# GLA decode moved three weight slabs forward, and the head norm spread over six gate slabs, in a one-core hybrid decoder step

## The chip, the cores and the metric

The kernel runs on one core of a Trainium2 chip. The metric is the device time of one execution in microseconds (us). The kernel before takes 2381.51 us, the median of three runs (2378.88 to 2381.75).

## What is computed

One layer of a hybrid decoder on 280 token columns: 256 prompt tokens, 8 sample tokens (one new token for each of 8 sequences) and 16 meta tokens. A half-step SwiGLU FFN, then two branches side by side, gated linear attention (GLA) and sliding-window attention, merged by two sigmoid gates, then a second FFN. What the change touches is GLA for the 8 sample tokens, and the norm behind it:

```python
# per sample token and head: one step of the recurrence on a state S (128 x 256), read and written back
S = S * exp(logg)[..., None] + k[:, None] * v[None, :]
o = q @ S
# head norm, gain, and gate r, for all tokens
of = o * lax.rsqrt(mean(o * o, axis=-1, keepdims=True) + EPS) * onorm
of = of * silu(r)
gla_b = of @ w_o
h = h + (sigmoid(ga + ba) * gla_b + sigmoid(gb + bb) * swa_b) @ w_out
```

All products with weights are done in three single-pass products of split operands (high times high, low times high, high times low).

## The kernel before

The work is a sequence of 404 weight **slabs**, one per 128 output columns, handled in a fixed order written out by hand for each engine. SyncE loads a slab's weights (1 MB, 16 tiles of 128x128) into one of two `raw` buffers. ScalarE rounds them to `w_hi` (`split_hi`, L458); VectorE subtracts to get `w_lo` (`split_lo`, L799); TensorE does 32 matmuls with `w_hi` (L1226, L1227: the high pass) and 16 with `w_lo` (L1232: the low pass); VectorE takes the result out of PSUM and frees the bank. There are two buffers of each kind, so the split for slab n+2 can only start when slab n has been multiplied:

```python
def split_hi(half, b, kt, first=False):          # called with half + 1 while slab (half, b) runs
    act.wait_ge(raw_loaded[b], 16 * (half + 1))
    if not first:
        act.wait_ge(slab_done, 2 * half + b - 1)
    act.activation(w_hi[:, b, 0:kt * P], raw[:, b, 0:kt * P], ACT.Copy).then_inc(hi_split, 1)
```

In the middle of the kernel stand 28 slabs that I number e = 8 to 35, as the changed code does. e = 8 to 15 are the rest of the GLA gate `ga`; e = 16 to 23 the output gate `r` (ScalarE `gate_r`, VectorE `silu_r`); e = 24 to 31 eight slabs of the merge gate `gb`; e = 32 to 35 four more. Then come twelve MERGE1 slabs, each half from the sliding-window output and half from the GLA output in `y3_hi`, `y3_lo`.

Beside e = 8 to 20 runs the chunked GLA of the prompt. Its small matmuls are issued by TensorE between the high and the low pass of a slab (`work_between`). ScalarE copies transposed value and key rows out of PSUM (`value_rows` L654, `key_rows` L658) and VectorE updates the state (`new_state` L1059, at e = 12, 17 and 20; semaphore `g_S` reaches 10 after the third).

The decode of the 8 sample tokens starts after slab e = 23. TensorE transposes the sample values (L1547), ScalarE and VectorE split them into `v_split`, and then token u goes beside slab e = 24 + u:

- ScalarE `pick_token` (L704) makes a selection tile for the token, one token ahead; L721 scales the four head states by the decay.
- TensorE broadcasts the token's values into two PSUM banks just before the slab (L1569, two matmuls of 512 columns). It waits there for the token's pick (`n_pick`) and for the state update of token u - 1 (`n_state`).
- VectorE adds key times value (L1103).
- TensorE multiplies state u by the query during the next slab (`decode_outputs` L1558, 8 products of one column), spread over the high pass; ScalarE copies the 8 columns out (L724).
- GpSimd loads and stores the 512 KB states, three buffers in turn (L418, L407).

After the last token ScalarE squares the outputs (L734). TensorE sums the squares over partitions in the slab e = 32 (L1583, L1584). ScalarE takes roots (L742), VectorE reciprocals (L1136) and the product with gain (L1118). GpSimd multiplies with `r` (L433). ScalarE and VectorE split the result into `y3_hi` (L747, L752) and `y3_lo` (L1124), which MERGE1 reads.

Of the kernel before, what the change touches and what calls it, by code (L numbers as in the profile page):

```python
# [21 lines left out]
ALU = mybir.AluOpType  # L22
# [5 lines left out]
P = 128  # L28
# [33 lines left out]


# [3 lines left out]
def build_layer(nc, t):  # L67
    ctx = ExitStack()
    with ctx:
# [16 lines left out]
        v_split, pick = small_r[0:32 + NS, 0:8 * P], small_r[0:32 + NS, 8 * P:].rearrange("p (a b) -> p a b", a=2)  # L86
# [93 lines left out]
        def by_block(a, h, side, n):  # L180
# [4 lines left out]
        S0 = R[:, 2112:2112 + 3 * GH * DV].rearrange("p (n h v) -> p n h v", n=3, h=GH)  # L185

        osq = [proj[:, 0:4, 0:TR], at(5216, 4, TR)]
        ostd, ors = at(4160, GH, TR), at(2112, GH, TR)
        ow, rsum = at(5216, 4, TR), proj[:, 0:4, 0:TR]
# [39 lines left out]
        state_out, nv_tr, nv_zero, nv_hi, nv_lo = (  # L229
            sem(n) for n in ("state_out", "nv_tr", "nv_zero", "nv_hi", "nv_lo"))  # L230
# [7 lines left out]
        on_sq, on_sum, on_std, on_rs, on_w, on_g, ohi_done, olo_done = (  # L238
            sem(n) for n in ("on_sq", "on_sum", "on_std", "on_rs", "on_w", "on_g", "ohi_done", "olo_done"))
# [36 lines left out]
        N_CONST = 10  # L276
# [3 lines left out]
        def _(sp):  # L280
# [19 lines left out]
            for dst, name in ((ones, "c_ones"), (ident, "c_ident"), (gbias, "gbias"),  # L300
                              (onorm, "onorm"), (nslope, "c_nslope"),
                              (a_bias, "a_bias"), (sink_bh, "sink_bh"), (pick_scale, "c_pick")):
                sp.dma_start(dst[:], t[name]).then_inc(consts_loaded, 16)
# [34 lines left out]
        def _(pool):  # L338
# [3 lines left out]
            for i in range(LEVELS):  # L342
# [6 lines left out]
                                   channel_multiplier=-1).then_inc(mask_fill, 1)  # L349

# [53 lines left out]
            def store_state(u):  # L404
                pool.wait_ge(n_state, 4 * (u + 1))
                pool.wait_ge(n_o, u + 1)
                pool.dma_start(t["state_s"][u], S0[:, u % 3]).then_inc(s0_stored[u % 3], 16)  # L407

            pool.wait_ge(g_chunk, 1)
            pool.dma_start(S0[:, 0], t["state_in"][0]).then_inc(s0_loaded[0], 16)  # L410
            pool.wait_ge(g_S, 10)
            pool.dma_start(t["state_p"], S).then_inc(state_out, 16)
            pool.wait_ge(state_out, 16)
            for u in range(1, NS):
                b = u % 3
                if u >= 3:
                    pool.wait_ge(s0_stored[b], 16 * (u // 3))
                pool.dma_start(S0[:, b], t["state_in"][u]).then_inc(s0_loaded[b], 16)  # L418
                if u >= 2:
                    store_state(u - 2)  # L420
# [32 lines left out]
        def _(act):  # L453
# [217 lines left out]
            for e in range(8, 24):  # L671
                half, b = GATE_A + e // 2, e % 2
                split_hi(half + 1, b, KD)
                act.wait_ge(bank_free, 2 * half + b + 1)
                if e < 16:
                    gate_a(half, slice(e, e + 1))
                else:
                    gate_r(e - 16)
                if e == 10:
                    for q in range(2):  # L680
                        value_rows(0, q)
                    key_rows(0)
                if e in (13, 14):
# [9 lines left out]
                if e == 19:  # L693
                    out_tiles(1)


            def gate_b(m):
                act.activation(merged[:, m], merged[:, m], ACT.Sigmoid, bias=gbias[:, 1, m:m + 1]).then_inc(sigb_done, 1)

            def pick_token(u):  # L700

                if u >= 2:
                    act.wait_ge(n_vbc, u - 1)
                act.activation(pick[:, u % 2], ones[0:32 + NS, :], ACT.Copy,  # L704
                               scale=pick_scale[0:32 + NS, u:u + 1]).then_inc(n_pick, 1)

            act.activation(v_split.rearrange("p (a b) -> p a b", a=8),
                           ones[0:32 + NS, :].unsqueeze(1).broadcast_to([32 + NS, 8, P]), ACT.Copy,
                           scale=0.0).then_inc(nv_zero, 1)
# [999 lines left out]
```

## Time and profile before

| | |
|---|---|
| median of 3 runs | 2381.51 us |
| profiled execution: its own time, its span | 2381.69 us, 2379.9 us |
| TensorE busy | 2335.3 us, 98% of the span |
| VectorE, ScalarE, GpSimd busy | 1290.0, 913.1, 165.7 us |
| mean granted TensorE clock | 0.987 |

Times in the profile are microseconds from the start of the span. PE is TensorE's matmul, DVE VectorE, ACT ScalarE, POOL GpSimd. The profile gives for every instruction its line, its start and duration, and, in brackets, how long the engine sat idle before it and which instruction ended that. PE's matmuls are pipelined, so their durations overlap; what counts is the distance between starts. The granted clock is the share of TensorE's full 2.4 GHz; 0.50 is its lower level, 1.2 GHz.

### The profile page before, as it was taken

How to read it: one execution, taken by the hardware profiler on the slowest of the kernel's cores; microseconds unless marked ns; L12 is line 12 of the kernel's file. 1: busy time of each engine (PE TensorE's matmuls, PEld its weight loads, DVE VectorE, ACT ScalarE, POOL GpSimd, SP SyncE). 2: the span in 40 equal slices, each digit the busy share in tenths (PEclk: the TensorE clock that was granted, in tenths of full speed). 3: DMA queues.
4: the chain of work that ended last, by engine and by line, in shares of the span. 5: the costliest groups of instructions: out<-in, count | busy, mean ns of one | idle time of the engine just before them, and what ended most of it. 6: DMA issues, size and time to landing. Idle time of an engine off the chain costs nothing.

```text
span 2379.9 us, 45022 instructions
## 1 busy us (share of the span) xinstructions
PE 2335.3 (98%) x18348; PEld 2302.7 (97%) x18348; DVE 1290.0 (54%) x1435; ACT 913.1 (38%) x935; POOL 165.7 (7%) x190
## 2 busy tenths in 40 slices
PE   8999999999999999999998989999999999999997
PEld 8999999999999999889998989999999999999997
DVE  6555554555555745554445565655555555555555
ACT  5333333333333434445234533443333333333332
POOL 0000000000000600001000120220000000000017
PEclk9999999999999999998899999999999999999999
DMA  5445444544544544335234545454455455545444
GB/s 204 174 152 183 176 160 161 191 161 159 188 163 158 183 163 160 109 127 191 95 132 181 203 149 179 175 179 176 174 177 192 176 170 192 183 161 195 177 171 147
DMA packets 66870, 401.56 MB, mean 169 GB/s; under 512 B 8530, under 2 KB 11218, under 8 KB 31456
## 3 DMA queue, kind: packets, MB, share of 16 engines
q1 hardware_dynamic: 61712, 385.73, 46.2%
q0 software_dynamic: 4032, 13.74, 1.7%
q8 instruction: 54, 0.88, 0.1%
q10 hardware_dynamic: 1056, 1.08, 0.1%
q14 instruction: 16, 0.13, 0.0%
HBM read 391.24 MB, written 9.27 MB: 168 GB/s over the span
## 4 chain that ended last, share of the span: by engine, by line
PE 95%; DVE 2%; ACT 1%; issue 1%; POOL 1%; DMA 0%; DVEq 0%; SPq 0%; ACTq 0%; POOLq 0%
PE bank L1226 30%; PE bank L1232 30%; PE bank L1227 30%; ACT w_hi L458 1%; DVE w_lo L799 1%; PE bank L1445 1%; PE bank L1365 0%; POOL scratch L433 0%; PE bank L1558 0%; PE bank L1363 0%; PE bank L1431 0%; PE bank L1430 0%; PE bank L1411 0%; DVE scratch L1136 0%; PE bank L1569 0%
## 5 line engine op out<-in xcount | busy, mean ns | idle before, releaser
L458 ACT ACTIVATE w_hi<-raw 128x2048 fp32r<-128x2048 f32 (+1 forms) x404 | 705.6, 1746 | 1274.5 <-PE bank L1232 1231.3
L799 DVE TENSOR_TENSOR w_lo<-raw,w_hi 128x2048 fp32r<-128x2048 f32 (+1 forms) x404 | 844.5, 2090 | 469.5 <-ACT w_hi L458 469.5
L1226 PE MATMUL bank<-x_hi,w_hi 128*128 128x264 f32 (+1 forms) x3440 | 886.0, 292 | 1.0 <-DVE x_lo L1165 1.0
L1227 PE MATMUL bank<-x_lo,w_hi 128*128 128x264 f32 (+1 forms) x3440 | 878.2, 289 | 0.0
L1226 PEld LDWEIGHTS bank<-x_hi,w_hi 128*128 128x128 f32 x3440 | 652.2, 190 | 11.6 <-issue 7.1
L1227 PEld LDWEIGHTS bank<-x_lo,w_hi 128*128 128x128 f32 x3440 | 652.1, 190 | 0.1
L1226 PE MATMUL bank<-y_hi,w_hi 128*128 128x264 f32 (+1 forms) x2368 | 597.8, 287 | 6.4 <-DVE y_lo L1124 5.9
L1227 PE MATMUL bank<-y_lo,w_hi 128*128 128x264 f32 (+1 forms) x2368 | 596.2, 287 | 0.0
L1232 PE MATMUL bank<-x_hi,w_lo 128*128 128x264 f32 (+1 forms) x3440 | 469.8, 288 | 0.0
L1226 PEld LDWEIGHTS bank<-y_hi,w_hi 128*128 128x128 f32 x2368 | 446.8, 189 | 7.7 <-DVE y_lo L1124 7.1
L1227 PEld LDWEIGHTS bank<-y_lo,w_hi 128*128 128x128 f32 x2368 | 447.5, 189 | 0.0
L1232 PEld LDWEIGHTS bank<-x_hi,w_lo 128*128 128x128 f32 x3440 | 445.5, 188 | 0.2
L1232 PE MATMUL bank<-y_hi,w_lo 128*128 128x264 f32 (+1 forms) x2368 | 322.5, 286 | 0.0
L1232 PEld LDWEIGHTS bank<-y_hi,w_lo 128*128 128x128 f32 x2368 | 303.2, 189 | 0.0
L858 DVE SCALAR_TENSOR_TENSOR hT<-bank,hT 128x280 f32 (+3 forms) x128 | 56.4, 441 | 116.9 <-PE bank L1232 116.6
L353 POOL MEMSET scratch<- 128x280 f32 x3 | 1.0, 334 | 1584.3 <-DVE scratch L831 1465.1
L831 DVE TENSOR_TENSOR scratch<-bank,rstd 128x280 f32<-128x280 f32 (+1 forms) x88 | 38.8, 441 | 129.5 <-PE bank L1232 129.5
L825 DVE TENSOR_TENSOR scratch<-bank,rstd 128x280 f32<-128x280 f32 (+1 forms) x88 | 38.8, 441 | 117.5 <-PE bank L1232 117.5
L359 POOL TENSOR_TENSOR scratch<-scratch 128x264 f32<-128x264 f32 (+1 forms) x47 | 74.4, 1583 | 3.7
L894 DVE SCALAR_TENSOR_TENSOR proj<-bank,rstd 128x280 f32<-128x280 f32 (+1 forms) x28 | 12.4, 442 | 58.5 <-PE bank L1232 58.4
L834 DVE TENSOR_TENSOR scratch<-scratch 128x280 f32<-128x280 f32 (+1 forms) x88 | 38.8, 441 | 3.0
L829 DVE TENSOR_TENSOR scratch<-scratch 128x280 f32<-128x280 f32 (+1 forms) x88 | 38.3, 436 | 1.0 <-ACT scratch L483 1.0
(252 smaller groups left out, 905.1 us busy)
## 6 DMA issues: line engine op xcount, KB each, us to landing
raw<-in_w_in SPq DMA_DIRECT2D x176, 1024.0 KB, 4.8
raw<-in_w_out SPq DMA_DIRECT2D x128, 704.0 KB, 4.1
raw<-in_w_proj SPq DMA_DIRECT2D x52, 1024.0 KB, 4.8
raw<-in_w_merge SPq DMA_DIRECT2D x32, 1024.0 KB, 4.8
raw<-in_w_o SPq DMA_DIRECT2D x16, 1024.0 KB, 4.8
scratch<-in_state_in POOLq DMA_DIRECT2D x8, 512.0 KB, 6.1
out_state_s<-scratch POOLq DMA_DIRECT2D x8, 512.0 KB, 5.3
hT<-in_xT SPq DMA_DIRECT2D x4, 560.0 KB, 7.3
```

What stands on the lines that cost most here:

```text
L359: pool.tensor_tensor(acc[:, 0:T], acc[:, 0:T], sq[:, 0:T], ALU.add).then_inc(acc_done, 1)
L458: act.activation(w_hi[:, b, 0:kt * P], raw[:, b, 0:kt * P], ACT.Copy).then_inc(hi_split, 1)
L799: dve.tensor_tensor(w_lo[:, b, 0:kt * P], raw[:, b, 0:kt * P], w_hi[:, b, 0:kt * P].bitcast(F32), ALU.subtract).then_inc(lo_split, 1)
L825: dve.tensor_tensor(a_n[:, 0:T], bank[own][:, 0:T], rstd[:, 0:T], ALU.mult).then_inc(bank_free, 1)
L829: dve.tensor_tensor(act_a[:, 0:T], a_n[:, 0:T], sig[:, 0:T], ALU.mult).then_inc(acta_done, 1)
L831: dve.tensor_tensor(b_n[:, 0:T], bank[own + 1][:, 0:T], rstd[:, 0:T], ALU.mult).then_inc(bank_free, 1)
L834: dve.tensor_tensor(s32[:, 0:T], act_a[:, 0:T], b_n[:, 0:T], ALU.mult).then_inc(s_done, 1)
L858: dve.scalar_tensor_tensor(hT[:, m, 0:T], bank[b][:, 0:T], 0.5, hT[:, m, 0:T], ALU.mult, ALU.add).then_inc(bank_free, 1)
L1226: pe.matmul(out, w, x[0][:, k, 0:T], start=(k == ks[0]), stop=False)
L1227: pe.matmul(out, w, x[1][:, k, 0:T], start=False, stop=False)
L1232: last = pe.matmul(out, w_lo[:, b, k * P:(k + 1) * P], x[0][:, k, 0:T], start=False, stop=(k == ks[-1]))
L1445: last = pe.matmul(bank[4 if i % 2 else 7][:, n * CK:(n + 1) * CK].rearrange("p (b x) -> p b x", x=h), proj[:, GK + g, c * CP:(c + 1) * CP ...
```

## The change

- **Start.** The loops over e = 8 to 23, over tokens and over the last four gate slabs become one loop over e = 8 to 35 on each engine. Token u now goes beside slab e = 21 + u (`DECODE = 21`).
- **Sample value rows.** The transposed tile of the meta tokens (columns 152 to 279) also holds the sample tokens, in partitions 104 to 111; at e = 10 it is split from there into `v_split`, now 128 partitions. The eight transposes L1547 go, and the `c_pick` table is made by three GpSimd instructions and no longer loaded.
- **ScalarE's order in a slab.** Decay of token u, then the weight split, then row copies, picks and outputs, then the gate.
- **States.** The three state buffers lie apart and are loaded as soon as their space is free.
- **Norm.** Token outputs are done in one piece between the passes. Each head's two squares are added on VectorE first, so TensorE's sums halve. They are done at e = 30, and roots, reciprocals, products and splits are spread over e = 30 to 35.

First, ScalarE beside a decode slab. Before (L698 gate, L704 pick, L721 decay, L724 token output, L458 weight split):

```order
L698 ACTIVATE proj<-proj,gbias 128x264 [waits bank_free]
L704 ACTIVATE small_r<-ones,pick_scale 40x128 [waits n_vbc]
L721 ACTIVATE scratch<-scratch,a_smp 128x256 [waits s0_loaded2]
L721 ACTIVATE scratch<-scratch,a_smp 128x256 x3
L724 ACTIVATE scratch<-bank 128x8 [waits n_o]
L458 ACTIVATE w_hi<-raw 128x2048 [waits slab_done,raw_loaded0]
L698 ACTIVATE proj<-proj,gbias 128x264 [waits bank_free]
```

And in the change (L695 decay, L465 weight split, L690 pick, L699 token output, L679 gate):

```order
L695 ACTIVATE scratch<-scratch,a_smp 128x256 [waits s0_loaded0]
L695 ACTIVATE scratch<-scratch,a_smp 128x256 x3
L465 ACTIVATE w_hi<-raw 128x2048 [waits slab_done,raw_loaded0]
L690 ACTIVATE small_r<-ones,pick_scale 128x128 [waits n_vbc]
L699 ACTIVATE scratch<-bank 128x8 [waits n_o]
L679 ACTIVATE proj<-proj,gbias 128x264 [waits bank_free]
```

The pick for the next token stood ahead of the weight split, which waits for the running slab, and now stands behind it.

Second, TensorE where the decode begins. Before, at the end of e = 23 (L1232 low pass, L1547 transposes of the sample values, L1569 broadcast of the first token's values):

```order
L1232 MATMUL bank<-x_hi,w_lo 128x264 [waits lo_split]
L1232 MATMUL bank<-x_hi,w_lo 128x264 x15
L1547 MATMUL bank<-ident,proj 8x128 [waits g_S,g_vtok]
L1547 MATMUL bank<-ident,proj 8x128 x7
L1569 MATMUL bank<-small_r 128x512 [waits n_pick,nv_lo]
L1569 MATMUL bank<-small_r 128x512
```

And in the change, at the end of e = 20 (L1503 keys by values for the last prompt chunk, L1248 low pass, L1573 broadcast):

```order
L1503 MATMUL bank<-scratch 128x256 [waits g_S,g_vtok,g_ktok]
L1503 MATMUL bank<-scratch 128x256 x3
L1248 MATMUL bank<-x_hi,w_lo 128x264 [waits lo_split]
L1248 MATMUL bank<-x_hi,w_lo 128x264 x15
L1573 MATMUL bank<-small_r 128x512 [waits g_S,nv_lo,n_pick]
L1573 MATMUL bank<-small_r 128x512
```

The transposes are gone, and the first broadcast, now three slabs earlier, waits itself for `g_S`. VectorE makes that count there, in the change, right behind its part of slab e = 20 (L1131 evacuation, L811 weight split, L1071 the third `new_state`, L1078 and L1080 `silu_r`):

```order
L1131 TENSOR_TENSOR r_act<-bank,rstd 128x264 [waits slab_done,rlo_done]
L811 TENSOR_TENSOR w_lo<-raw,w_hi 128x2048 [waits hi_split]
L1071 SCALAR_TENSOR_TENSOR scratch<-scratch,a_chunk,bank 128x256 [waits g_S,g_o,g_chunk,g_kv]
L1071 SCALAR_TENSOR_TENSOR scratch<-scratch,a_chunk,bank 128x256 x3
L1078 TENSOR_TENSOR r_act<-r_act,gadT 128x264 [waits r_sig]
```

This order is as before; only what waits for it has moved. The core of the diff:

```diff
+DECODE, NORM = 21, 30
...
# ScalarE
-            for e in range(8, 24):
+            for e in range(8, 36):
                 half, b = GATE_A + e // 2, e % 2
+                u = e - DECODE
+                if 0 <= u < NS:
+                    decay_state(u)
                 split_hi(half + 1, b, KD)
-                act.wait_ge(bank_free, 2 * half + b + 1)
-                if e < 16:
-                    gate_a(half, slice(e, e + 1))
-                else:
-                    gate_r(e - 16)
...
                 if e == 18:
                     for q in range(2):
                         value_rows(2, q)
                     key_rows(2)
                 if e == 19:
+                    act.wait_ge(pick_fill, 3)
+                    pick_token(0)
                     out_tiles(1)
+                if 0 <= u < NS - 1:
+                    pick_token(u + 1)
+                if 0 < u <= NS:
+                    token_out(u - 1)
+                if u == NS:
+                    head_squares()
+                if e == NORM:
+                    head_roots()
+                if e > NORM + 1:
+                    branch_hi(e - NORM - 2)
                 act.wait_ge(bank_free, 2 * half + b + 1)
-                gate_b(8 + u)
+                if e < 16:
+                    gate_a(half, slice(e, e + 1))
+                elif e < 24:
+                    gate_r(e - 16)
+                else:
+                    gate_b(8 + e - 24 if e < 32 else 4 + e - 32)
...
# VectorE, behind the evacuation and split of each slab
+                if e == NORM - 1:
+                    head_sums()
+                if e in (NORM, NORM + 1):
+                    for g in range(2):
+                        head_inverse(2 * (e - NORM) + g)
...
+                    gated_norm(e - NORM)
+                if e > NORM + 1:
+                    branch_lo(e - NORM - 2)
+                    if e - NORM < GH:
+                        gated_norm(e - NORM)
...
# TensorE, between the passes of a slab
+                    if DECODE < e <= DECODE + NS:
+                        for n in range(8):
+                            decode_outputs(e - DECODE - 1, n)
+                    if e == NORM:
+                        head_norms()
...
+            def broadcast_values(u):
+
+                pe.wait_ge(n_pick, u + 1)
+                if u == 0:
+                    pe.wait_ge(nv_lo, 2)
+                    pe.wait_ge(g_S, 10)
+                else:
+                    pe.wait_ge(n_state, 4 * u)
...
+            for e in range(8, 36):
+                if DECODE <= e < DECODE + NS:
+                    broadcast_values(e - DECODE)
+                slab(GATE_A + e // 2, e % 2, KD, x, TR, beside=work_between(e))
```

## Rows read from the trace of the kernel before

**Rows 1.** The page: the chain that ended last, shares by engine.

```profile
PE 95%; DVE 2%; ACT 1%; issue 1%; POOL 1%; DMA 0%; DVEq 0%; SPq 0%; ACTq 0%; POOLq 0%
```

**Rows 2.** Waits of TensorE, whole span: us in total, times, longest.

```profile
PE bank L1226 <- DVE y_lo L1124: 5.9, 3, 3.6
PE bank L1500 <- ACT scratch L654: 2.4, 1, 2.4
PE bank L1342 <- ACT scratch L574: 2.3, 1, 2.3
```

**Rows 3.** Timeline, PE: first matmuls of slabs e = 19, 20, 21 (start, duration).

```profile
1227.24 0.28 PE L1226 MATMUL bank<-x_hi,w_hi 128*128 128x264 f32 x1
...
1240.87 0.28 PE L1226 MATMUL bank<-x_hi,w_hi 128*128 128x264 f32 x1
...
1248.43 0.28 PE L1226 MATMUL bank<-x_hi,w_hi 128*128 128x264 f32 x1
```

**Rows 4.** Timeline, DVE: evacuations of e = 15, 16, 23, 24, 25; split and new_state in e = 20.

```profile
1203.28 0.43 DVE L1075 TENSOR_TENSOR proj<-bank,rstd 128x264 f32<-128x264 f32 x1 [1.28 <-PE bank L1232]
...
1212.72 0.43 DVE L1075 TENSOR_TENSOR r_act<-bank,rstd 128x264 f32<-128x264 f32 x1 [5.14 <-PE bank L1232]
...
1250.64 2.29 DVE L799 TENSOR_TENSOR w_lo<-raw,w_hi 128x2048 fp32r<-128x2048 f32 x1 [1.51 <-ACT w_hi L458]
1252.85 1.65 DVE L1059 SCALAR_TENSOR_TENSOR scratch<-scratch,a_chunk,bank 128x256 f32<-128x256 f32 x4
...
1266.29 0.43 DVE L1075 TENSOR_TENSOR r_act<-bank,rstd 128x264 f32<-128x264 f32 x1 [0.37 <-PE bank L1232]
...
1283.53 0.43 DVE L1107 TENSOR_TENSOR proj<-bank,rstd 128x264 f32<-128x264 f32 x1 [5.74 <-PE bank L1232]
...
1292.00 0.43 DVE L1107 TENSOR_TENSOR proj<-bank,rstd 128x264 f32<-128x264 f32 x1 [2.60 <-PE bank L1232]
```

**Rows 5.** Timeline, ACT: split and row copies at e = 18; pick; split at e = 30.

```profile
1227.50 1.92 ACT L458 ACTIVATE w_hi<-raw 128x2048 fp32r<-128x2048 f32 x1 [0.54 <-PE bank L1232]
...
1232.45 1.06 ACT L654 ACTIVATE scratch<-bank 128x512 f32<-128x512 f32 x2
...
1328.18 0.39 ACT L704 ACTIVATE small_r<-ones,pick_scale 40x128 fp32r<-40x128 f32 x1
...
1334.43 1.91 ACT L458 ACTIVATE w_hi<-raw 128x2048 fp32r<-128x2048 f32 x1 [1.91 <-PE bank L1232]
```

**Rows 6.** Timeline, PE: the first broadcast, and the one before slab e = 31.

```profile
1274.88 1.22 PE L1569 MATMUL bank<-small_r 40*128 40x512 f32 x2 [7.82 <-DVE small_r L1096]
...
1334.26 0.73 PE L1569 MATMUL bank<-small_r 40*128 40x512 f32 x2
1334.92 0.39 PE L1226 MATMUL bank<-x_hi,w_hi 128*128 128x264 f32 x1
```

**Rows 7.** Timeline, PE: the last token's outputs, then starts up to the third MERGE1 slab.

```profile
1342.65 1.84 PE L1558 MATMUL bank<-proj,scratch 128*128 128x1 f32 x16
...
1350.29 0.61 PE L1583 MATMUL bank<-proj,ones 128*128 128x264 f32 x2
...
1353.65 0.48 PE L1226 MATMUL bank<-x_hi,w_hi 128*128 128x264 f32 x1
...
1365.57 0.28 PE L1226 MATMUL bank<-x_hi,w_hi 128*128 128x264 f32 x1
...
1371.44 0.28 PE L1226 MATMUL bank<-y_hi,w_hi 128*128 128x264 f32 x1
...
1393.01 0.28 PE L1226 MATMUL bank<-y_hi,w_hi 128*128 128x264 f32 x1
```

**Rows 8.** Stretches: length, PE busy (count), granted clock, DMA share, GB/s.

```profile
1233.00:1240.00 7.00, 6.34 (x41) 0.76 0.37 145
919.00:926.00 7.00, 6.66 (x50) 0.76 0.40 152
...
1502.00:1506.00 4.00, 2.96 (x24) 1.00 0.00 0
```

More of the change, by code:

```diff
@@ L669, in gate_r, with gate_b, sample_values_hi, pick_token @@
                 act.activation(y3_hi[:, m], r_act[:], ACT.Copy).then_inc(rhi_done, 1)
-            for e in range(8, 24):
+            def gate_b(m):
+                act.activation(merged[:, m], merged[:, m], ACT.Sigmoid, bias=gbias[:, 1, m:m + 1]).then_inc(sigb_done, 1)
+            def sample_values_hi():
+                for q in range(2):
+                    act.activation(v_split[96:P, 512 * q:512 * q + 512], rows_bank(0, q)[96:P, :], ACT.Copy).then_inc(nv_hi, 1)
+            def pick_token(u):
+                if u >= 2:
+                    act.wait_ge(n_vbc, u - 1)
+                act.activation(pick[:, u % 2], ones[:], ACT.Copy, scale=pick_scale[:, u:u + 1]).then_inc(n_pick, 1)
@@ L682, in _ @@
                     key_rows(0)
+                    act.wait_ge(nv_zero, 1)
+                    sample_values_hi()
                 if e in (13, 14):
@@ L1144, in _ @@
-            gated_norm(GH - 1)
-            branch_lo(GH - 1)
+                if e == 8:
+                    dve.wait_ge(att_zero, 1)
+                    for c in range(NCP):
+                        pick_diagonal(c)
+                if e < 8 + LEVELS:
+                    pick_level(e - 8)
+                if e == 10:
+                    for q in range(2):
+                        sample_values_lo(q)
+                if e == 7 + LEVELS:
+                    dve.tensor_copy(a_chunk[:], dec[CP]).then_inc(g_chunk, 1)
@@ L1538, in between @@
                             keys_to_rows(2, h)
[L1539 to L1548 removed]
+                    if DECODE < e <= DECODE + NS:
+                        for n in range(8):
+                            decode_outputs(e - DECODE - 1, n)
+                    if e == NORM:
+                        head_norms()
+                return between
+            def broadcast_values(u):
+                pe.wait_ge(n_pick, u + 1)
+                if u == 0:
+                    pe.wait_ge(nv_lo, 2)
+                    pe.wait_ge(g_S, 10)
+                else:
+                    pe.wait_ge(n_state, 4 * u)
+                for q in range(2):
+                    last = pe.matmul(bank[4 + q][:], pick[:, u % 2], v_split[:, 512 * q:512 * q + 512], start=True, stop=True)
+                last.then_inc(n_vbc, 1)
             def decode_outputs(u, n):
```

234 lines of the change are left out of this document (89 added, 145 removed).

## The prediction

> **What bounds the kernel.** I read the page first: the chain that ended last lies on TensorE for 95% of the span [rows 1]. Such a kernel gets faster only where TensorE idles, runs at the lower clock, or has less to do. The list of TensorE's waits comes second: it is short, and two of its entries stand in the part that the change rewrites, the waits for the row copies L654 and for the last splits L1124 [rows 2]; the wait before the first broadcast is the third [rows 6]. So the rest is read from starts on TensorE and VectorE. A plain slab takes 1371.44 - 1365.57 = 5.87 us [rows 7], a broadcast 1334.92 - 1334.26 = 0.66 [rows 6]. The sum below runs from the start of slab e = 19 (1227.24) to the third MERGE1 slab (1393.01) [rows 3, 7]; outside it I find nothing that moves TensorE. I work against the profiled execution (2381.69 us), which is 0.2 above the median 2381.51; the sum is a difference, so I set it on the median.
>
> **The clock** has to be priced before the sum. Two waits of 2.4 and 2.3 us [rows 2] were each followed by a stretch at the lower of TensorE's two levels: 7 us around each ran at a mean granted clock of 0.76, which loses 7 x 0.24 = 1.7 us of full-speed work each time [rows 8]. A wait of about 1.0 us drew no drop (4.00 - 2.96 idle, clock 1.00) [rows 8]. After the wait of 7.82 us the broadcast and slab e = 24 took from 1274.88 to the evacuation at 1283.53, 8.65 us [rows 4, 6], against 0.66 + 5.87 = 6.53 plus 0.1 of lag to the evacuation: 2.0 us.
>
> **What goes away.**
> - Row copies ahead of the gate. Slab e = 19 took 1240.87 - 1227.24 = 13.63 us [rows 3]; e = 16, with the same extra matmuls and no wait, 1212.72 - 1203.28 = 9.44 [rows 4]. In the change the two copies (1.06) follow ScalarE's split, which ended at 1227.50 + 1.92 = 1229.42 [rows 5]: ready at 1230.5, and TensorE's high pass ends two thirds of 5.87 after 1227.24, at 1231.2. Gain 4.2, with 0.7 to spare.
> - The old start of the decode: from evacuation e = 23 to e = 24 passed 17.24 us [rows 4], and 6.53 would do. Gain 10.7; this holds the transposes, the wait and its clock.
> - Token outputs in one piece: a slab with the eight interleaved took 1292.00 - 1283.53 = 8.47 [rows 4]; with 16 weight loads in a row ahead of it, 1350.29 - 1342.65 = 7.64, so 1.77 over a plain one [rows 7]. 8.47 - 0.66 - 7.64 = 0.17, seven times: 1.2.
> - Half of the norm sums: 1353.65 - 1350.29 = 3.36 [rows 7], gain 1.7.
> - The tail: e = 35 ends at 1371.44, and two MERGE1 slabs take until 1393.01, 21.57 us instead of 11.74 [rows 7]. In the change the roots, reciprocals and splits start two slabs earlier and each VectorE step ends before TensorE needs it, up to the last two splits, which come in about as TensorE asks. I leave 0.5 there: gain 9.3.
>
> Together 27.1 us. The removed table load, three small GpSimd instructions and the 128-partition tiles stand beside other work; nothing on TensorE waits for them. If that cover went, they would cost under 1 us.
>
> **What is added.**
> - The first broadcast waits for `g_S` = 10. The last `new_state` sits in VectorE's part of e = 20, behind ScalarE's split and VectorE's own (2.29): it ended at 1252.85 + 1.65 = 1254.50, while e = 20 ended on TensorE at 1248.43 [rows 3, 4]. Before, nothing needed it for three more slabs; now TensorE stands 6.1 us, in front of slab e = 21. With the clock's 2.0: 8.1.
> - The picks. Before, a token's pick was copied while the slab ahead of its broadcast ran. Now it stands behind the weight split for slab n + 2, and that one waits for the end of slab n. ScalarE's split began at 1334.43 and ended at 1336.34, when TensorE had gone on at 1334.26 [rows 5, 6]; a pick takes 0.39 [rows 5]. So the pick comes 1336.34 + 0.39 - 1334.26 = 2.5 us after the end of each slab, and TensorE's next instruction is the broadcast that needs it. Token 0 is made ahead (e = 19); tokens 1 to 7 pay: 7 x 2.5 = 17.3. Each wait is as long as the two that drew the lower clock, so 1.7 more each, 11.8. The unknown is this clock: 0 below, 2.0 each above (14.0); I take 1.7, from the two waits of nearest length. Together 29.1.
> - The norm sums now wait between the passes of e = 30. VectorE reaches the sums of squares after both splits of that slab (about 0.2 + 1.91 + 2.29 = 4.4 us after the end of e = 29, from [rows 4, 5]), TensorE asks at two thirds of 5.87, 3.9. With one addition of 0.43 (as an evacuation of the same size [rows 4]) ahead of the first sum that is 0.9; the state store that must land first could make it 2. I take 1.0.
>
> Together 38.2. Behind ScalarE's pick are queued the token output and the gate of the same slab; neither is late for anyone at a slab of 0.66 + 5.87 + 1.77 + 2.5 + 1.7 = 12.5 us. The state loads get more time per token than they had, so no wait for a DMA takes their place.
>
> **Sum.** 38.2 - 27.1 = 11.1 us slower: 2381.5 + 11.1 = **2392.6 us**, slower by 0.47%. About 0.2% (4.8 us) is what a measurement of this kernel can tell from no change.
>
> **A rule that speaks otherwise.** Both 2.3 us waits cost clock in this trace [rows 2, 8]. The Trainium skill, page "TensorE: Matmul & The Clock Gate", section "HAM oscillation — how this bites in real kernels", says that TensorE has to idle for longer than these waits last before its clock falls; by that the seven picks would cost their 17.3 us alone. The trace speaks against it, twice in two; but two waits are few.
>
> **The rivals.**
> - *The seven waits are there, but the clock holds.* For it: one wait of 1.0 us without a drop, and seven short ones are not two. The time is 2392.6 - 11.8 = 2380.8, no change. If three or fewer of the seven drop, the result is still within 0.2%. The rule above is this rival. Chance 0.19.
> - *The picks are never late.* One mechanism: ScalarE's split runs a slab ahead of TensorE, so that the pick behind it is done before the slab ends. It decides once ScalarE is more than 2.5 us ahead. Then 29.1 us fall away: 2363.5, faster. For it: the names of the semaphores in the order show no counts. Against: the split of 1334.43 idled 1.91 us and was released by the low pass of the running slab [rows 5], and so were the splits of the other decode slabs. Chance 0.08. This is also the case where the change does what it says, a decode that begins three slabs sooner at no cost but the `g_S` wait.
> - *The lower clock lasts from one wait to the next.* Then each of seven slabs runs at half speed through 0.66 + 5.87 + 1.77 = 8.3 us instead of losing 1.7: 7 x 6.6 = 46 more, 2439. Against: after each wait of the trace the clock was back within 7 us [rows 8]. Chance 0.03.
> - *The tail keeps its wait*, because a state store or GpSimd is late for the norm: 9.3 of gain lost, 2402. Chance 0.04.
>
> **How the numbers follow.** The forecast has 0.66. Its own range: the clock of four to seven drops at 1.7 to 2.0 gives 2387 to 2395, and the norm wait and tail add up to 3: 2398. The no-drop case, with waits of 2.1 instead of 2.5, reaches down to 2379. So 2379 to 2398 holds the forecast and the first rival, and leaves out some 0.15. Faster by over 0.2%: the second rival and a little of the first, 0.10. Slower by over 0.2%: forecast, third and fourth, and a little off for three drops, 0.71. The rest, 0.19, is no change.
>
> **What would show it.** In the profile of the changed kernel: TensorE waits for a pick (`small_r` from ScalarE) seven times, 2.3 to 2.5 us each, and once about 6 us for VectorE's state update; the two waits for L654 and L1124 are gone or under 1 us; starts of broadcasts 12.5 us apart in e = 22 to 28; a granted clock near 0.86 there. No waits for picks would make the forecast wrong by its largest term; waits at full clock would make it the first rival.

## The result

The changed kernel takes 2386.28 us, the median of 20 runs, against 2381.62 for the kernel before (20 runs): +4.7 us, ratio 1.0018 with a 95% interval of 1.0012 to 1.0025. One of the 20 lasted 7861 us and is left out of the ratio; the others lie between 2381.43 and 2387.95. The forecast was +11.1. The sign and the range held it, the size was less than half.

The profiled execution took 2382.57 us, span 2380.8, mean granted clock 0.989. The chain that ended last still lies on TensorE, where [rows 1] had 95%. The line is the page's, after:

```profile
PE 94%; DVE 2%; ACT 2%; issue 1%; DMA 0%; DVEq 0%; SPq 0%; ACTq 0%; POOLq 0%
```

TensorE's waits between 1200 and 1400 us, the changed kernel (waiting operation, what it waits for, us in total, times, longest):

```profile
PE bank L1573 <- ACT small_r L690: 16.5, 7, 2.4
PE bank L1573 <- DVE scratch L1071: 6.0, 1, 6.0
PE bank L1593 <- DVE scratch L1102: 1.6, 1, 1.6
PE bank L1242 <- DVE y_lo L1122: 0.9, 1, 0.9
```

This answers [rows 2]: the waits for the row copies and the 5.9 us for the last splits are gone or down to 0.9, and in their place stand the waits that the forecast named, seven for a pick and one for the third `new_state`. Now the broadcasts, from TensorE's timeline after (start, duration, and in brackets the idle time ahead):

```profile
1247.24 1.20 PE L1573 MATMUL bank<-small_r 128*128 128x512 f32 x2 [6.04 <-DVE scratch L1071]
1257.61 1.22 PE L1573 MATMUL bank<-small_r 128*128 128x512 f32 x2 [2.35 <-ACT small_r L690]
1269.69 0.74 PE L1573 MATMUL bank<-small_r 128*128 128x512 f32 x2 [2.35 <-ACT small_r L690]
1281.95 0.74 PE L1573 MATMUL bank<-small_r 128*128 128x512 f32 x2 [2.35 <-ACT small_r L690]
1292.67 0.73 PE L1573 MATMUL bank<-small_r 128*128 128x512 f32 x2 [2.35 <-ACT small_r L690]
1303.38 0.73 PE L1573 MATMUL bank<-small_r 128*128 128x512 f32 x2 [2.35 <-ACT small_r L690]
1314.10 0.74 PE L1573 MATMUL bank<-small_r 128*128 128x512 f32 x2 [2.35 <-ACT small_r L690]
1326.34 0.74 PE L1573 MATMUL bank<-small_r 128*128 128x512 f32 x2 [2.35 <-ACT small_r L690]
```

Seven equal waits, but not seven equal slabs. The distances from token 1 on are 12.08, 12.26, 10.72, 10.71, 10.72 and 12.24 us; the slab of token 7, by VectorE's evacuations at 1324.03 and 1334.75, takes 10.72. So 10.7 is a slab with a wait at full clock, and three slabs (those of tokens 1, 2 and 6) take 1.4 to 1.5 more. The stretches of slabs e = 23 to 28 show why (columns as in [rows 8], with all engines: PE, PEld, DVE, ACT, POOL busy, then the granted clock, DMA share, GB/s):

```profile
1267.00:1279.00 12.00, 9.65 (x66) 9.34 (x66) 5.16 (x8) 4.60 (x9) 1.07 (x2) 0.86 0.46 173
1279.00:1290.00 11.00, 8.65 (x70) 8.34 (x70) 5.16 (x8) 4.60 (x9) 1.07 (x2) 1.00 0.52 195
1290.00:1301.00 11.00, 8.65 (x69) 8.18 (x67) 4.30 (x6) 4.27 (x8) 1.07 (x2) 1.00 0.56 202
1301.00:1311.70 10.70, 8.35 (x67) 8.07 (x66) 4.30 (x6) 4.27 (x8) 1.07 (x2) 1.00 0.61 197
1311.70:1324.00 12.30, 9.94 (x67) 9.58 (x66) 4.29 (x6) 4.27 (x8) 1.07 (x2) 0.86 0.48 173
1324.00:1334.70 10.70, 8.36 (x68) 8.26 (x69) 4.30 (x6) 4.27 (x8) 0.53 (x1) 1.00 0.40 147
```

The mean clock is 0.86 where a slab is long and 1.00 where it is not. Behind three of the seven waits TensorE ran for a while at its lower level (called a fall below), behind four it did not.

The whole stretch, after: ScalarE's weight splits behind slab e = 18 and behind the second MERGE1 slab (each starts when the slab has been multiplied), and TensorE's first matmuls of the first and the third MERGE1 slab:

```profile
1224.29 1.92 ACT L465 ACTIVATE w_hi<-raw 128x2048 fp32r<-128x2048 f32 x1 [0.54 <-PE bank L1248]
...
1380.93 0.28 PE L1242 MATMUL bank<-y_hi,w_hi 128*128 128x264 f32 x1
...
1393.91 0.28 PE L1242 MATMUL bank<-y_hi,w_hi 128*128 128x264 f32 x1
...
1394.17 1.92 ACT L465 ACTIVATE w_hi<-raw 128x2048 fp32r<-128x2048 f32 x1 [3.99 <-PE bank L1248]
```

The two MERGE1 slabs that took 21.57 us in [rows 7] take 1393.91 - 1380.93 = 12.98. From ScalarE's split behind slab e = 18 (1224.29, where [rows 5] has 1227.50) to 1394.17, where the kernel before stood at 1393.27, are 169.88 us against 165.77: +4.1. Ahead of slab e = 8 the code is the same, yet the profiled execution of the change is 3.2 us ahead there: its clock between 1080 and 1160 us was 0.91 and 0.83, that of before 0.87 and 0.79. Such differences come and go between executions of one kernel, and the profiled execution is 3.7 below its median; the stretch, not the span, is what compares.

### The profile page after: what moved, and what is told of

Read it like the earlier page. It is cut to its first block, busy times and chain, and to the rows that moved or that the text cites. A ratio compares the mean times of both kernels' runs of the same rounds, so it can differ in the third digit from the quotient of the medians.

```text
span 2380.8 us, 44998 instructions
## 1 busy us (share of the span) xinstructions
PE 2327.5 (98%) x18332; PEld 2298.1 (97%) x18332; DVE 1292.9 (54%) x1439; ACT 912.2 (38%) x935; POOL 169.9 (7%) x193
## 4 chain that ended last, share of the span: by engine, by line
PE 94%; DVE 2%; ACT 2%; issue 1%; DMA 0%; DVEq 0%; SPq 0%; ACTq 0%; POOLq 0%
PE bank L1242 30%; PE bank L1243 30%; PE bank L1248 30%; ACT w_hi L465 1%; DVE w_lo L811 1%; PE bank L1583 1%; PE bank L1461 1%; PE bank L1381 0%; PE bank L1379 0%; PE bank L1447 0%; PE bank L1446 0%; PE bank L1573 0%; DMA out_state_s<-scratch 0%; PE bank L1427 0%; PE bank L1278 0%
## 5 line engine op out<-in xcount | busy, mean ns | idle before, releaser
L465 ACT ACTIVATE w_hi<-raw 128x2048 fp32r<-128x2048 f32 (+1 forms) x404 | 705.6, 1747 | 1305.5 <-PE bank L1248 1248.2
L811 DVE TENSOR_TENSOR w_lo<-raw,w_hi 128x2048 fp32r<-128x2048 f32 (+1 forms) x404 | 844.1, 2089 | 466.5 <-ACT w_hi L465 466.5
L1248 PE MATMUL bank<-x_hi,w_lo 128*128 128x264 f32 (+1 forms) x3440 | 470.2, 289 | 0.0
L1248 PEld LDWEIGHTS bank<-x_hi,w_lo 128*128 128x128 f32 x3440 | 445.6, 189 | 0.2
L1248 PE MATMUL bank<-y_hi,w_lo 128*128 128x264 f32 (+1 forms) x2368 | 321.8, 286 | 0.0
L1248 PEld LDWEIGHTS bank<-y_hi,w_lo 128*128 128x128 f32 x2368 | 302.4, 188 | 0.0
```

Source lines behind the costliest of these rows:

```text
L811: dve.tensor_tensor(w_lo[:, b, 0:kt * P], raw[:, b, 0:kt * P], w_hi[:, b, 0:kt * P].bitcast(F32), ALU.subtract).then_inc(lo_split, 1)
L1248: last = pe.matmul(out, w_lo[:, b, k * P:(k + 1) * P], x[0][:, k, 0:T], start=False, stop=(k == ks[-1]))
```

## Experiments

**Is it the picks?** First the pick goes back ahead of the weight split, in the changed kernel:

```diff
                 if 0 <= u < NS:
                     decay_state(u)
+                if 0 <= u < NS - 1:
+                    pick_token(u + 1)
                 split_hi(half + 1, b, KD)
...
-                if 0 <= u < NS - 1:
-                    pick_token(u + 1)
```

> The changed kernel with one part undone: the pick for the next token stands ahead of the weight split again. Theory A (the seven waits cost their 16.5 us, and each lowers the clock only in some executions, three in seven in the one profiled, about half on the mean, 1.5 us each): 2386.3 - 16.5 - 5.3 = 2364.5, and the runs lie as close together as those of before. Theory B (each of the seven waits always costs 1.7 of clock, as predicted): 2386.3 - 16.5 - 11.8 = 2358. Theory C (the short waits never cost clock, what differs between runs comes from elsewhere): 2369.8, and the runs spread as in the changed kernel, by 6.5 us. All: no wait of TensorE for a pick.

Measured: 2363.82 us (2362.27 to 2365.79), ratio to before 0.9928 [0.9915, 0.9942]. All TensorE waits of that kernel between 1200 and 1400 us:

```profile
PE bank L1573 <- DVE scratch L1071: 6.0, 1, 6.0
PE bank L1593 <- DVE scratch L1102: 1.6, 1, 1.6
PE bank L1242 <- DVE y_lo L1122: 0.9, 1, 0.9
```

The seven waits are gone, and slabs e = 22 to 28 take 8.09 us each. A wait at full clock therefore costs 10.72 - 8.09 = 2.63 and the seven 18.4; three falls of 1.5 add 4.6: 23.0, where the medians differ by 22.5. That is near Theory A's sum; its guess that the falls come in some executions only does not hold, as the repeats below show. One line in the wrong place turns 17 us of gain into a loss of 4.7.

**Short and long waits.** If the clock falls after a wait, its length should matter. Below, the pick waits for the end of the slab by itself, and stands ahead of the weight split:

```diff
+                if 0 <= u < NS - 1:
+                    act.wait_ge(slab_done, 2 * half + b + 1)
+                    pick_token(u + 1)
                 split_hi(half + 1, b, KD)
```

> The pick stands ahead of the weight split but waits for the end of the running slab itself, so that the seven waits are there and short: about 0.2 + 0.39 = 0.6 us each. Theory A (a short wait does not lower the clock, as the 1.0 us wait of the trace of before): the pick-ahead version plus 7 x 0.6 = 4.2, about 2368.7, no low clock in slabs e = 22 to 28. Theory B (any wait there lowers the clock): 7 x 1.7 = 12 more, 2380.

2366.69 us, ratio 0.9939 [0.9926, 0.9953]: seven waits of 0.5 us, slabs of 8.85, no fall. And longer ones, by six more ScalarE copies ahead of each pick:

```diff
                 if 0 <= u < NS - 1:
+                    for idle in (*(a_up[:, i * P:i * P + P] for i in range(4)), at(6400, P), at(6528, P)):
+                        act.activation(idle, ones[:], ACT.Copy)
                     pick_token(u + 1)
```

> The changed kernel with six copies of 0.3 us on ScalarE ahead of each of the seven picks, into tiles that nobody reads, so that each wait is about 4.2 us instead of 2.4. Theory A (the longer the wait, the surer the fall of the clock): all seven fall; 2386.3 + 7 x 1.8 = 2398.9, and 5 us more for the falls that the changed kernel misses, 2404; runs closer together than in the changed kernel. Theory C (the length does not matter): 2398.9 and the same spread.

2399.44 us, ratio 1.0080 [1.0066, 1.0094]; the waits came out at 3.55 us each, not the 4.2 expected. The broadcasts of tokens 2 to 4:

```profile
1272.51 0.73 PE L1575 MATMUL bank<-small_r 128*128 128x512 f32 x2 [3.55 <-ACT small_r L690]
1285.91 0.73 PE L1575 MATMUL bank<-small_r 128*128 128x512 f32 x2 [3.55 <-ACT small_r L690]
1297.80 1.22 PE L1575 MATMUL bank<-small_r 128*128 128x512 f32 x2 [3.55 <-ACT small_r L690]
```

13.40 and then 11.89: the wait of token 3, no shorter than the others, drew no fall, and the other six did. The time lies near Theory C's 2398.9 only because the waits were shorter than planned: 7 x 1.2 more of waiting and three more falls of 1.5 make 2399.2. Longer waits fall more often (none of seven at 0.5, three at 2.35, six at 3.55), but length alone does not decide.

**Which waits fall?** Twice more the changed kernel as it is:

> The changed kernel once more, for its clock. Theory A (the fall depends on when a wait happens to come, not on its length): again seven waits of 2.35 us, the clock down behind two to four of them and not behind the same three tokens (1, 2 and 6 in the first trace); median near 2386. Rival (some tokens' waits always lower the clock, since more stands idle around them): the same three.

2385.47 us (2383.14 to 2390.14), ratio 1.0022 [1.0013, 1.0031], slabs e = 22 to 28: 12.18, 12.23, 10.70, 10.71, 10.72, 12.23, 10.72.

> The changed kernel unaltered, a third look at which of the seven equal waits are followed by a low clock. If it depends on the place of each wait in the program's time, slabs e=22, 23 and 27 take 12.2 us again and the other four 10.7; if it depends on how the program's start falls against something else on the chip, other slabs do, still about three of seven.

2387.70 us in its one run; 12.18, 12.24, 10.72, 10.70, 10.72, 12.25, 10.72. Three profiles, and three times tokens 1, 2 and 6, although the decode began up to 2.4 us earlier or later within the span. (Here the wait for the norm sums, 2.5 us, was also followed by a fall: e = 30 took 12.02 us instead of 9.43. That, 2.6 us, and a start of the decode 2.4 us later are nearly all of the 5.1 us between the two profiled executions.) So it is no chance. Either the place in the program decides, or what TensorE did before. Two kernels leave one set each, with the pick (the "sampling step" of the expectations from here on) early for the tokens named and late for the rest. This is the first; the second has (3, 4, 5, 7) in both lines:

```diff
+                if 0 <= u < NS - 1 and u + 1 in (1, 2, 6):
+                    pick_token(u + 1)
                 split_hi(half + 1, b, KD)
...
-                if 0 <= u < NS - 1:
+                if 0 <= u < NS - 1 and u + 1 not in (1, 2, 6):
                     pick_token(u + 1)
```

> The changed kernel with the sampling step of tokens 1, 2 and 6 alone ahead of the weight split: those were the three whose wait was followed by a low clock, in all three profiles of the changed kernel. The waits of tokens 3, 4, 5 and 7 stay, 4 x 2.35. Theory (whether a wait drops the clock goes with its place, and these four places hold it): no slab over 10.8 us, slabs of 8.1 and 10.7, some 2386 - 3 x 2.6 - 4.6 = 2374 us. Rival (it goes with what TensorE did just before, so that another wait drops when its forerunners are gone): one or two of the four take 12.2, 2375 to 2377 us.

2377.82 us (2377.07 to 2381.24), ratio 0.9988 [0.9978, 0.9997]. Broadcasts of tokens 2 to 7, and the evacuations around the slab of token 7:

```profile
1265.70 0.62 PE L1575 MATMUL bank<-small_r 128*128 128x512 f32 x2
1276.30 0.73 PE L1575 MATMUL bank<-small_r 128*128 128x512 f32 x2 [2.35 <-ACT small_r L690]
1287.01 0.73 PE L1575 MATMUL bank<-small_r 128*128 128x512 f32 x2 [2.35 <-ACT small_r L690]
1299.25 0.73 PE L1575 MATMUL bank<-small_r 128*128 128x512 f32 x2 [2.35 <-ACT small_r L690]
1307.44 0.62 PE L1575 MATMUL bank<-small_r 128*128 128x512 f32 x2
1318.05 0.73 PE L1575 MATMUL bank<-small_r 128*128 128x512 f32 x2 [2.35 <-ACT small_r L690]
...
1315.73 0.43 DVE L1133 TENSOR_TENSOR proj<-bank,rstd 128x264 f32<-128x264 f32 x1 [2.22 <-PE bank L1250]
...
1327.93 0.43 DVE L1133 TENSOR_TENSOR proj<-bank,rstd 128x264 f32<-128x264 f32 x1 [6.33 <-PE bank L1250]
```

From token 4 to token 5 pass 12.24 us, and the evacuations of the last slab lie at 1315.73 and 1327.93, 12.20 apart. The waits of tokens 4 and 7, which held the clock in all three profiles of the changed kernel, were now followed by a fall. The wait for the norm sums, 2.0 us here, was too (e = 30: 11.47 us), 2.0 more than behind a wait at full clock (9.43).

> The other way round: tokens 3, 4, 5 and 7 ahead of the weight split, so that the waits of 1, 2 and 6 alone stay, 3 x 2.35. Theory (the place decides): slabs e=22, 23 and 27 take 12.2 us again, the others 8.1, some 2386 - 4 x 2.6 = 2375.5 us. Rival (what came just before decides): the wait of token 6, now behind four slabs without one, draws no drop, or those of 1 and 2 alone keep theirs: 2374 us with a slab e=27 of 10.7.

2374.02 us (2369.74 to 2376.17), ratio 0.9969 [0.9956, 0.9981]. Broadcasts of tokens 1 to 7:

```profile
1260.49 1.22 PE L1575 MATMUL bank<-small_r 128*128 128x512 f32 x2 [2.35 <-ACT small_r L690]
1272.67 0.74 PE L1575 MATMUL bank<-small_r 128*128 128x512 f32 x2 [2.35 <-ACT small_r L690]
1282.39 0.62 PE L1575 MATMUL bank<-small_r 128*128 128x512 f32 x2
1290.48 0.62 PE L1575 MATMUL bank<-small_r 128*128 128x512 f32 x2
1298.58 0.62 PE L1575 MATMUL bank<-small_r 128*128 128x512 f32 x2
1309.18 0.73 PE L1575 MATMUL bank<-small_r 128*128 128x512 f32 x2 [2.35 <-ACT small_r L690]
1317.38 0.62 PE L1575 MATMUL bank<-small_r 128*128 128x512 f32 x2
```

Tokens 1 and 2 fell as before (12.18; and 9.72 to a broadcast that does not wait), token 6 no longer: 8.20 follow it. In both kernels the rival of the expectation holds: the place of a wait of 2.35 us in the program does not decide whether it costs clock, and taking away other waits changes it. Taking them away also brings the later waits forward (token 4's ends at 1287.01 in the first of the two kernels, at 1292.67 in the changed kernel), and these runs do not separate what ran before a wait from the moment at which it comes. A shift of the whole decode by up to 2.4 us, as between the three profiles, changed nothing by itself. By what rule waits are followed by a fall is open.

**The state update.** The third `new_state` ahead of VectorE's evacuation in e = 20, in the changed kernel:

```diff
+                if e == 20:
+                    new_state(2)
                 dve.wait_ge(slab_done, 2 * half + b + 1)
...
-                if e in (12, 17, 20):
-                    new_state((12, 17, 20).index(e))
+                if e in (12, 17):
+                    new_state((12, 17).index(e))
```

> The changed kernel with the third state update ahead of the evacuation in slab e = 20, and nothing else. Theory A: the 6.0 us wait and the clock behind it go, 14.0 us for slab e = 21 become about 6.5: 2386.3 - 7.5 = 2378.8, and the seven waits for picks stay, 16.5 us, with the clock down behind some of them. Rival: the wait is only moved, since ScalarE's gate and decay of e = 20 and 21 come late too: less than 3 us of gain.

2376.62 us (11 runs), ratio 0.9983 [0.9974, 0.9992]. The 6.0 us are gone and e = 21 takes 7.21 instead of 13.99; the 16.5 us for the picks stay. Against the changed kernel measured beside it (2385.47) that is 8.9 us, of which e = 21 is 6.8 in the traces. Their falls moved to other tokens here too (slabs 11.57, 10.72, 12.23, 10.71, 10.70, 10.72, 12.26: part of one behind token 1, then tokens 3 and 7). Both edits together:

> As the one before, and the third state update of the prompt moved ahead of the evacuation of slab e = 20 on VectorE, so that it is done before the slab ends. All theories: the 6.0 us wait of the first broadcast goes, and with it the low clock behind it (14.06 us for slab e = 21 instead of 6.53): 7.5 us less than the run before, 2357 under theory A. Rival: VectorE is busy there and the evacuation comes late, then only part of the 7.5.

2354.92 us (4 runs), ratio 0.9894 [0.9879, 0.9909]. What is left on TensorE is 1.6 us for the norm sums, 0.9 for a state addition and 0.9 for a split. The norm sums wait because VectorE reaches them late and then for a store, as its timeline in the changed kernel shows:

```profile
1344.39 2.29 DVE L811 TENSOR_TENSOR w_lo<-raw,w_hi 128x2048 fp32r<-128x2048 f32 x1 [1.58 <-ACT w_hi L465]
1347.22 0.78 DVE L1102 TENSOR_TENSOR scratch<-proj 128x264 f32<-128x264 f32 x2 [0.54 <-DMA out_state_s<-scratch]
```

The last version moves them up as well: the last token's output and its squares ahead of ScalarE's split at e = 29, and VectorE's sums in place in the squares' own tile, so that the wait for the store can stand later, ahead of the reciprocals:

```diff
+                if u == NS:
+                    token_out(u - 1)
+                    head_squares()
                 split_hi(half + 1, b, KD)
...
+                if e == NORM - 1:
+                    head_sums()
                 dve.wait_ge(slab_done, 2 * half + b + 1)
...
-                    dve.tensor_tensor(osum[:, h], sq2[:, h % 2 * 2], sq2[:, h % 2 * 2 + 1], ALU.add).then_inc(on_add, 1)
+                    dve.tensor_tensor(sq2[:, h % 2 * 2], sq2[:, h % 2 * 2], sq2[:, h % 2 * 2 + 1], ALU.add).then_inc(on_add, 1)
```

> The run with the sampling step ahead of the split and the third state update moved (2354.9 us), and at slab e=29 the last token's output and its squares ahead of the split on ScalarE, the squares' sums ahead of the slab's evacuation on VectorE, with the wait for the stored state put off to where the norm is inverted. Theory: the wait of 1.6 us for the norm sums goes and nothing takes its place: about 2353 us. Rival (the evacuation of e=29 comes late instead, by the sums' own time): 2355 us or a little more.

2353.78 us (2350.32 to 2354.77, 4 runs), ratio 0.9883 [0.9869, 0.9897]. Two waits remain:

```profile
PE bank L1576 <- DVE scratch L1094: 1.0, 1, 1.0
PE bank L1245 <- DVE y_lo L1123: 0.9, 1, 0.9
```

Slabs e = 29 and 30 take 8.44 + 6.81 = 15.25 by the evacuations, against 7.63 + 9.51 = 17.14 without this edit: 1.9 in the trace. In the medians it is 1.1, and the ranges of the two overlap, so of the last step only the trace speaks. The version is some 27 us faster than the kernel before.

**The row copies alone**, in the kernel before: `value_rows` and `key_rows` ahead of the gate.

```diff
                 split_hi(half + 1, b, KD)
-                act.wait_ge(bank_free, 2 * half + b + 1)
-                if e < 16:
-                    gate_a(half, slice(e, e + 1))
-                else:
-                    gate_r(e - 16)
...
                 if e == 19:
                     out_tiles(1)
+                act.wait_ge(bank_free, 2 * half + b + 1)
+                if e < 16:
+                    gate_a(half, slice(e, e + 1))
+                else:
+                    gate_r(e - 16)
```

> The kernel before with the row copies and output copies of e = 10 to 19 ahead of the gate, and nothing else. Theory A: the wait of 2.35 us in slab e = 19 and the low clock behind it go: 13.63 us become 9.44, 2381.6 - 4.2 = 2377.4. Rival: the gate that is now later holds up VectorE and gives it back: 2381.6.

2378.05 us (11 runs), ratio 0.9988 [0.9979, 0.9997]. The wait is gone and e = 19 takes 9.44 us in place of 13.63, the 4.2 of the forecast; the medians show 2.7 of them, and the interval, 0.7 to 5.0 us, holds both.

**The pick alone**, in the kernel before: `pick_token` from ahead of the weight split to behind it.

```diff
-                if u + 1 < NS:
-                    pick_token(u + 1)
...
                 split_hi(half + 1, b, KD)
+                if u + 1 < NS:
+                    pick_token(u + 1)
```

> The kernel before with the pick for the next token behind the weight split instead of ahead of the decay, and nothing else. Theory A: seven waits of TensorE, 2.6 us of slab time each as between the changed kernel and the one with the pick ahead (10.72 and 8.09), and about three falls of the clock at 1.5: 2381.6 + 18.4 + 4.6 = 2404.6. Theory B (every wait costs 1.7 of clock): 2411.9. Rival (the waits belong to the earlier start, where ScalarE has the output gate to do): 2381.6.

2441.20 us (2426.55 to 2442.98), ratio 1.0241 [1.0216, 1.0266], 37 us beyond the expectation. The waits are the same as in the changed kernel, 7 x 2.35, but the broadcasts of tokens 2 to 4 lie 17.1 us apart:

```profile
1301.27 1.12 PE L1569 MATMUL bank<-small_r 40*128 40x512 f32 x2 [2.35 <-ACT small_r L704]
1318.36 1.14 PE L1569 MATMUL bank<-small_r 40*128 40x512 f32 x2 [2.35 <-ACT small_r L704]
1335.44 1.15 PE L1569 MATMUL bank<-small_r 40*128 40x512 f32 x2 [2.35 <-ACT small_r L704]
```

and the stretch of one slab has 14.65 us of TensorE at a mean clock of 0.60 (columns as above):

```profile
1302.00:1319.00 17.00, 14.65 (x67) 13.89 (x66) 4.21 (x7) 4.31 (x9) 1.07 (x2) 0.60 0.34 124
```

Here the lower clock lasted through most of each slab, seven times: the third rival of the prediction, on another kernel than it was meant for. One thing that differs beside the slabs is that a token's eight products of one column stand strewn among the full-width products of the high pass here, and in one piece in the changed kernel. So: the same kernel with them in one piece,

```diff
-                     beside=(lambda i: decode_outputs(u - 1, i // 2) if i % 2 and i < 16 else None) if u else None)
+                     beside=(lambda i: [decode_outputs(u - 1, n) for n in range(8)] if i == KD - 1 else None) if u else None)
```

> The kernel before with the sampling step behind the weight split (as in the run of that step alone, 2441 us), and the decode products of a token issued in one piece. Theory (strewn products keep the clock low after a wait): the seven waits of 2.35 us stay, slabs of 10.7, two to four of them 12.2, in place of 17.1: about 2381 + 18.4 + 3 to 6 - 1.2, some 2402 us. Rival (the low clock came from the kernel before itself, or from the step's place): slabs stay near 17 us, about 2440 us.

2410.63 us (2403.04 to 2413.08), ratio 1.0130 [1.0115, 1.0145]: 31 us faster than with them strewn, and 9 over the expectation. The profiled execution took 2403.04, near the expected 2402; the other three took 2410.6 to 2413.1, and what they add is in no trace. Broadcasts of tokens 2 to 5:

```profile
1294.85 0.73 PE L1569 MATMUL bank<-small_r 40*128 40x512 f32 x2 [2.35 <-ACT small_r L704]
1305.76 0.73 PE L1569 MATMUL bank<-small_r 40*128 40x512 f32 x2 [2.35 <-ACT small_r L704]
1318.20 1.22 PE L1569 MATMUL bank<-small_r 40*128 40x512 f32 x2 [2.35 <-ACT small_r L704]
1331.95 0.73 PE L1569 MATMUL bank<-small_r 40*128 40x512 f32 x2 [2.35 <-ACT small_r L704]
```

10.91, 12.44, 13.75: the waits are as before, and the mean clock of the seven slabs is 0.75 to 1.00 in place of 0.60. In this kernel the strewn products keep the clock down. And the other way round, the changed kernel with its products strewn:

```diff
                 def between(i):
+                    if DECODE < e <= DECODE + NS and i % 2 and i < 16:
+                        decode_outputs(e - DECODE - 1, i // 2)
                     if i != KD - 1:
                         return
...
-                    if DECODE < e <= DECODE + NS:
-                        for n in range(8):
-                            decode_outputs(e - DECODE - 1, n)
```

> The changed kernel, but the sixteen one-column decode products of a token are issued one by one between the bands of the high pass again, as the kernel before does, not in one piece. Theory (products strewn among the bands keep the clock low once a wait has dropped it): slabs e=22 to 28 take about 17 us each in place of 10.7 to 12.2, the granted clock near 0.5 in them, about 45 us in all: some 2430 us. Rival (one piece saves only its 0.2 us per slab): slabs of 10.9 to 12.4, some 2387 us.

2401.89 us, ratio 1.0101 [1.0076, 1.0125], between the two expectations. The runs form two groups, 2395.0 to 2395.4 and 2408.4 to 2413.1. In the profile, which is of the faster group, the broadcasts of tokens 3 and 4 lie 15.38 apart, nearly the 17 of the kernel before with late picks, and the others 10.7 to 12.3. Below them stands a wait that the changed kernel does not have, of a strewn product at e = 29 for ScalarE's token output:

```profile
1282.55 0.74 PE L1572 MATMUL bank<-small_r 128*128 128x512 f32 x2 [2.35 <-ACT small_r L690]
1297.93 1.22 PE L1572 MATMUL bank<-small_r 128*128 128x512 f32 x2 [2.35 <-ACT small_r L690]
...
PE bank L1582 <- ACT scratch L699: 1.7, 1, 1.7
```

Slab e = 29 takes 14.04 us behind it, at a mean clock of 0.65, where it took 7.63: 6.4 of the 12.5 us by which this execution is longer than the profiled one of the changed kernel. So strewn products make a low clock last longer in both kernels, in one all through and in the other in two slabs of the trace. Why the changed kernel comes out of it and the other does not was not found; the two differ in more than this, for instance in the broadcast, of 40 rows in one and 128 in the other.

The trace of the kernel before, further up, shows that the clock can fall without any wait. From 1122 to 1137 us TensorE issues products of 8 columns (L1430, L1431) and waits for nothing. From 1126 to 1137 the granted clock is 0.50, and from 1143, among the full-width products that follow, it is 1.00 again. A stretch of it (columns as above):

```profile
1130.00:1135.00 5.00, 5.00 (x21) 4.76 (x20) 0.00 (x0) 0.00 (x0) 0.00 (x0) 0.50 0.25 103
```

The changed kernel does the same there (0.50 from 1125 to 1137). So idle time is not the only thing that lowers the clock: here it fell while TensorE did narrow products. That the strewn products keep it down in the same way fits this, but no run shows it.

## Why the forecast was right in kind and wrong in size

The forecast's sum was right part by part, but for one term. Slabs are measured from evacuation to evacuation.

| step of the prediction | forecast | measured |
|---|---|---|
| e = 19, row copies ahead of the gate | 9.44 us | 9.44 |
| first broadcast waits for `g_S` | 6.1 + 2.0 clock | 6.04 + 1.4 clock (e = 21: 13.99) |
| seven picks, the waits | 7 x 2.5 = 17.3 | 7 x 2.35 of idling; by slabs 7 x 2.63 = 18.4 |
| **seven picks, the clock** | **7 x 1.7 = 11.8** | **3 x 1.5 = 4.6** |
| outputs in one piece, e = 29 | 7.64 | 7.63 |
| norm sums, e = 30 | 5.87 + 1.7 + 1.0 = 8.55 | 9.43 |
| two MERGE1 slabs | 11.74 + 0.5 | 12.98 |

**The step that failed** is "Each wait is as long as the two that drew the lower clock, so 1.7 more each, 11.8". Two waits of this length, both followed by a fall [rows 8], were taken as the price of all seven, though the prediction itself called two waits few. Of seven waits of 2.35 us three fell, the same three in every profile, and the price per fall was nearly right (1.5; the 1.7 took the 7 us of [rows 8] whole, of which TensorE was busy 6.34 and 6.66). The term was 7.2 us too high, more than the whole error of 6.4. The other terms nearly cancel: each of the seven slabs at full clock is 10.72 where the sum had 0.66 + 5.87 + 1.77 + 2.5 = 10.80, together 0.6 less; e = 21 is 0.6 less (13.99 against 14.63, the clock behind the first wait); the norm sums 0.9 more, since the store that the prediction feared held VectorE 0.54, and a wait costs the slab 0.3 beyond its own length, as behind the picks (2.63 for 2.35); the merge slabs 0.7 more. Why three of the seven fell, and not all or none, stays open. Without the falls behind the picks the stretch would have shown +4.1 - 4.6 = -0.5, where the forecast without its 11.8 had -0.7.

**The first rival**, waits at full clock, was half of what happened: four of seven. Its text said that with three or fewer falls the result would still be within 0.2%, and it is, at 0.18%: by the prediction's own bound the result is the "no change" to which it gave 0.19. The Trainium skill, page "TensorE: Matmul & The Clock Gate", section "HAM oscillation — how this bites in real kernels", would have had no fall behind any of these waits. The two stretches at 0.86 and the slabs of 12 us speak against it, as [rows 8] did; that four of seven held does not bear it out, since two of the four fell once other waits had been taken away.

**The second rival**, picks never late, did not come, since every split waited for the running slab; its time is what the run with the pick ahead of the split gives: 2363.82, forecast 2363.5. **The third**, a low clock that lasts, came only with the products strewn. The prediction priced the products in one piece at 1.2 us of gain, from slab times of the kernel before. There, where TensorE has no waits between tokens, that was fair; beside the late picks they are worth 31 us there (2441.20 - 2410.63). In the changed kernel the medians differ by 16 (2401.89 - 2386.28), between two groups of runs, and in the profiled execution half of it is the new wait at e = 29 and what follows it. The fourth did not come: the tail's wait shrank to 0.9.

**Where the large gain went.** Of the 27 us that the forecast removes, 26 went: all of them but 0.7 at the tail. They were given back mainly at two places, both of the same kind: a small producer on a side engine put behind a weight split that waits for TensorE itself. The experiments take both back and reach 2354.92, and with the norm sums 2353.78.

## What to carry to other kernels

When work moves to an earlier place, look at what its producers stand behind on their own engines: here a copy of 0.38 us behind a weight split that waits for the running slab cost TensorE 2.6 us per token and a fall at three of seven, and the same line ahead of the split cost nothing. Price an idle gap of TensorE at its length plus a clock term that is a range, from nothing to the dearest fall in the trace per gap, and put several equal gaps in the middle of that range unless a run with as many of them is at hand. Where gaps cannot be avoided, keep narrow products in one piece rather than strewn among the wide ones.

## What was not expected of the hardware

- Equal waits of 2.35 us were followed by the lower clock in three of seven cases, and the same three in three profiles. Taking away the waits of others changed which ones (tokens 4 and 7 fell once 1, 2 and 6 did not wait; 6 no longer fell once 3, 4, 5 and 7 did not). Waits of 0.5 us drew none, six of seven of 3.55 us did.
- One-column products among wide ones kept the clock at a mean of 0.60 for seven slabs in a row behind such waits, 17.08 us a slab; the same products in one piece let it come back, 10.9 to 13.8 us a slab. That the strewn products alone do this is not shown: in the kernel before, without late picks, they run at 8.47 us a slab [rows 4].
- While TensorE did products of 8 columns, with no wait among them, the clock went from 1.00 to 0.50 (1126 to 1137 us in the kernel before).
